# First modulation weights by feature tile: eight pieces with places of their own, four up0 units loaded early, their high parts cast on ScalarE

## The reference

```python
sc = jax.nn.silu(c)
scc = jax.nn.silu(c_ctx)
for layer in range(DEPTH):
    mod_l = (sc @ ada_w[layer] + ada_b[layer]).reshape(-1, N_MOD, D_MODEL)[:, :, None, :]
    mod_c = (scc @ ada_w[layer] + ada_b[layer]).reshape(N_MOD, D_MODEL)
    x_l = half_ffn(x_l, mod_l[:, 0], mod_l[:, 1], mod_l[:, 2], norm_g[layer, 0], ...)
    ...
def half_ffn(x, shift, scale, gate, g, w_gate, w_up, w_down):
    h = rmsnorm(x, g) * (1 + scale) + shift
    return x + 0.5 * gate * swiglu(h, w_gate, w_up, w_down)
```

## Time and profile before

| | us |
|---|---|
| median of 3 runs (lowest, highest) | 2646.4 (2646.07, 2648.47) |
| profiled execution, whole time | 2649.49 |
| profiled execution, span from first to last instruction | 2647.7 |
| TensorE busy in the span | 2518.1 (95%) |
| VectorE, ScalarE busy | 1554.8 (59%), 485.1 (18%) |
| mean transfer rate | 135 GB/s |

### The profile page before, as it was taken

One profiled execution on the slowest core, in us unless ns is written; L12 is line 12 of the kernel. 1 busy time (PEld: TensorE's weight loads), 2 busy tenths in 40 slices (PEclk: granted clock), 3 DMA queues, 4 the chain that ended last, 5 costly groups with the idle time before them and its releaser, 6 DMA issues.

```text
span 2647.7 us, 38248 instructions
## 1 busy us (share of the span) xinstructions
PE 2518.1 (95%) x15322; PEld 2142.3 (81%) x15322; DVE 1554.8 (59%) x2396; ACT 485.1 (18%) x991; POOL 5.0 (0%) x12
## 2 busy tenths in 40 slices
PE   5999999999999999999999789998999999799998
PEld 2777777877777777788888659998988999799997
DVE  4544434434644443655544637888687766679976
ACT  2000000124200000211100242111156522210001
POOL 0000000000000000000000000000000000000000
PEclk9999999999999999999999899998999999899999
DMA  5554555310354545333223204655443222346553
GB/s 206 196 183 163 178 176 192 96 32 25 124 186 161 182 167 183 104 103 96 97 94 98 82 19 127 190 179 164 163 149 107 96 65 81 120 143 187 184 185 107
DMA packets 88990, 356.81 MB, mean 135 GB/s; under 512 B 9825, under 2 KB 11105, under 8 KB 79393
## 3 DMA queue, kind: packets, MB, share of 16 engines
q1 hardware_dynamic: 86976, 349.32, 39.7%
q0 software_dynamic: 848, 4.67, 0.5%
q10 hardware_dynamic: 1040, 1.05, 0.1%
HBM read 353.95 MB, written 1.05 MB: 134 GB/s over the span
## 4 chain that ended last, share of the span: by engine, by line
PE 90%; DVE 6%; ACT 2%; DMA 2%; issue 1%; SPq 0%; DVEq 0%; ACTq 0%
PE lin L1927 24%; PE lin L1928 23%; PE lin L1929 23%; PE pair L2030 3%; PE pair L2111 2%; DMA raw_all<-w_ada 2%; PE lin L2138 1%; PE lin L1976 1%; DVE work L1500 1%; PE lin L1977 1%; PE lin L1980 1%; PE pair L2496 1%; PE pair L2483 1%; PE lin L1935 1%; PE lin L1937 1%
## 5 line engine op out<-in xcount | busy, mean ns | idle before, releaser
L1927 PE MATMUL lin<-h_all,whi 128*128 128x256 f32 (+1 forms) x2608 | 872.9, 335 | 11.1 <-DVE wlo L1423 6.1
L1928 PE MATMUL lin<-h_all,whi 128*128 128x256 f32 (+1 forms) x2608 | 860.8, 330 | 0.0
L1929 PE MATMUL lin<-h_all,wlo 128*128 128x256 f32 (+1 forms) x2608 | 860.1, 330 | 0.0
L1423 DVE TENSOR_TENSOR wlo<-raw_all,whi 128x1024 fp32r<-128x1024 f32 (+1 forms) x529 | 635.8, 1202 | 36.1 <-ACT whi L1270 19.1
L1927 PEld LDWEIGHTS lin<-h_all,whi 128*128 128x128 f32 x2608 | 497.0, 191 | 96.9 <-issue 44.9
L1422 DVE CAST whi<-raw_all 128x1024 fp32r<-128x1024 f32 (+2 forms) x489 | 330.8, 676 | 400.4 <-PE lin L1929 357.9
L1929 PEld LDWEIGHTS lin<-h_all,wlo 128*128 128x128 f32 x2608 | 497.1, 191 | 45.1
L1928 PEld LDWEIGHTS lin<-h_all,whi 128*128 128x128 f32 x2608 | 497.5, 191 | 42.6
L1927 PE MATMUL lin<-a_all,whi 128*128 128x256 f32 (+1 forms) x1148 | 388.6, 339 | 23.8 <-DVE wlo L1423 10.9
L1928 PE MATMUL lin<-a_all,whi 128*128 128x256 f32 (+1 forms) x1148 | 384.6, 335 | 0.0
L1929 PE MATMUL lin<-a_all,wlo 128*128 128x256 f32 (+1 forms) x1148 | 384.2, 335 | 0.0
(11 more groups left out here) (317 smaller groups left out, 2021.3 us busy)
## 6 DMA issues: line engine op xcount, KB each, us to landing
raw_all<-w_up SPq DMA_DIRECT2D x176, 512.0 KB, 3.5
raw_all<-w_ada SPq DMA_DIRECT2D x72, 1024.0 KB, 4.9
raw_all<-w_down SPq DMA_DIRECT2D x64, 512.0 KB, 3.5
raw_all<-w_exp_up SPq DMA_DIRECT2D x64, 512.0 KB, 3.6
raw_all<-w_exp_down SPq DMA_DIRECT2D x32, 512.0 KB, 3.5
raw_all<-w_down SPq DMA_DIRECT2D x32, 384.0 KB, 3.0
raw_all<-w_b_qk SPq DMA_DIRECT2D x24, 512.0 KB, 3.5
raw_all<-w_b_conv SPq DMA_DIRECT2D x24, 512.0 KB, 3.5
```

Source lines behind the costliest of these rows:

```text
L1423: dve.tensor_tensor(wlo[s][:, 0:n], r[:, 0:n], whi[s][:, 0:n].bitcast(F32), ALU.subtract)\
L1927: pe.matmul(out_, a, hi[n], start=start and n == 0, stop=False)
L1928: pe.matmul(out_, a, lo[n], start=False, stop=False)
L1929: ins = pe.matmul(out_, b, hi[n], start=False, stop=stop and n == len(cols) - 1)
```

## The change

Group 0 is laid out anew in HBM. Piece f (1 MB) holds, for all eight input tiles, the 128 shift columns and the 128 scale columns of feature tile f. So each piece gives the whole shift and scale of one tile. The eight pieces go to eight places in the working area that later holds the feed-forward's inner values (`first_block`), and no load of them waits. The four first up0 units go to the four places of `raw_all`, among the pieces: after piece 0 units 0 and 1, after piece 2 unit 2, after piece 5 unit 3. `x` comes in two transfers. All other pairs use the two upper places as before.

`sum_block(f)` replaces the group's sums: eight matmuls with 32 columns of weights (`cond`, padded with zeros to 32) and 256 moving columns, two in each of four groups of 32 partitions. ScalarE copies 128 x 256 (`copy_block`). `turn_block` is two matmuls that add the four partition groups and turn the row in one step (`same_row` picks the rows). VectorE makes bias and gain of the tile in two small steps (`first_modulations`). Three PSUM banks take turns, and the row buffer's two halves too. ScalarE casts the high parts of units 0 to 3 (`first_high`), VectorE makes the low parts (`first_low`), at places in the norm written out by hand.

```diff
-            sp.dma_start(x[:, :, :], dram["x_t"]).then_inc(S("x_in"), 16)
-            for p in range(8):
-                load_pair(sp, p)
+            for part, name in enumerate(("x_in", "x_rest_in")):
+                k = slice(part * KT // 2, (part + 1) * KT // 2)
+                sp.dma_start(x[:, k, :], dram["x_t"][:, k, :]).then_inc(S(name), 16)
+            for f in range(8):
+                sp.dma_start(first_block(f), dram["w_ada"][f]).then_inc(block_loaded[f], 16)
+                for j in {0: (0, 1), 2: (2,), 5: (3,)}.get(f, ()):
+                    load_unit(sp, "up0", 0, j)
...
@@ ScalarE: norm_root, norm_high, start @@
+                if src == "load":
+                    copy_block(0)
                 act.activation(small[:, 16:17], ones[:, 0:1], ACT.Sqrt)
...
                     ins.then_inc(S("h_hi_ready"), 1)
+                    if ph == "ffn0":
+                        if k == 0:
+                            first_high(2)
+                        if k + 2 < 8:
+                            copy_block(k + 2)
+                        if k == 4:
+                            first_high(3)
+            def first_high(j):
+                act.wait_ge(raw_loaded[j], 16)
+                act.activation(whi[j][:, :], raw[j], ACT.Copy).then_inc(S("first_high"), 1)
+            def copy_block(f):
+                act.wait_ge(S("block_summed"), f + 1)
+                if f >= 2:
+                    act.wait_ge(S("block_turned"), f - 1)
+                act.activation(ada_row[:, SEQ * (f % 2):SEQ * (f % 2 + 1)], block_bank(f)[:, 0:SEQ], ACT.Copy)\
+                    .then_inc(S("block_copied"), 1)
...
             norm_root("ffn0")
-            copy_modulations(0)
+            first_high(0)
+            first_high(1)
+            copy_block(1)
@@ VectorE @@
-            split("up0", 0, 0)
-            dve.wait_ge(S("params_in"), 32)
-            take_modulations(0)
-            for j in range(1, LOOK):
-                split("up0", 0, j)
+            def first_modulations(f):
+                dve.wait_ge(S("block_turned"), f + 1)
+                at = slice(f, f + KT + 1, KT)
+                src = view(block_bank(f)[:, SEQ:SEQ + 4], (2, 2))
+                link(dve.tensor_tensor(mods[:, at, :], src, P_("ada_b")[:, at].unsqueeze(2).broadcast_to([P, 2, 2]), ALU.add))
+                link(dve.scalar_tensor_tensor(gains[:, 0, f, :], mods[:, KT + f, :], 1.0,
+                                              P_("norm_g")[:, f:f + 1].broadcast_to([P, 2]), ALU.add, ALU.mult))
+                dve.sem_inc(S("block_modulated"), 1)
+            def first_low(j):
+                dve.wait_ge(S("first_high"), j + 1)
+                dve.tensor_tensor(wlo[j][:, :], raw[j], whi[j][:, :].bitcast(F32), ALU.subtract).then_inc(weights_split, 1)
+            def beside_first_norm(t):
+                if t == 0:
+                    first_low(1)
+                    first_modulations(1)
+                    first_low(2)
+                elif t < KT - 1:
+                    first_modulations(t + 1)
+                if t == 5:
+                    first_low(3)
...
+            first_modulations(0)
+            first_low(0)
@@ TensorE @@
+            def sum_block(f):
+                pe.wait_ge(block_loaded[f], 16)
+                if f >= 3:
+                    pe.wait_ge(S("block_modulated"), f - 2)
+                for half in range(2):
+                    for g in range(4):
+                        k = 2 * g + half
+                        ins = pe.matmul(block_bank(f)[32 * g:32 * g + 32, 0:SEQ], cond[:, k, :],
+                                        first_block(f)[:, SEQ * k:SEQ * (k + 1)], start=half == 0, stop=half == 1)
+                ins.then_inc(S("block_summed"), 1)
+            def turn_block(f):
+                pe.wait_ge(S("block_copied"), f + 1)
+                for m in range(2):
+                    at = SEQ * (f % 2) + P * m
+                    ins = pe.matmul(block_bank(f)[:, SEQ + 2 * m:SEQ + 2 * m + 2], ada_row[:, at:at + P], same_row[:, :],
+                                    start=True, stop=True)
+                ins.then_inc(S("block_turned"), 1)
+            def blocks_beside(k):
+                if k + 2 < 8:
+                    turn_block(k + 2)
+                if k + 3 < 8:
+                    sum_block(k + 3)
...
-            for p in range(8):
-                sum_modulations(p)
+            sum_block(0)
             norm("ffn0")
-            turn_modulations(0)
+            sum_block(1)
+            turn_block(1)
+            sum_block(2)
```

More of the change, by code:

```diff
@@ L90, in load_order @@
 def load_order():
-    order = [("pair", p) for p in range(8)]
+    order = []
     for name, n, _, _ in STREAM:
@@ L109, in load_plan @@
         if name == "pair":
-            b = j % 2 if j < 8 else 1
-            slots = (2 * b, 2 * b + 1)
+            slots = (2, 3)
         else:
-            slots = ((POSITION[name][1] + j) % 2 if name in POSITION else (FIRST[name] + j) % SLOTS,)
+            slots = (j if name == "up0" and j < 4 else (POSITION[name][1] + j) % 2 if name in POSITION else (FIRST[name] + j) % SLOTS,)
         waits = sorted({holder[q] for q in slots if holder[q]})
@@ L123 @@
 PLAN = load_plan()
-PAIR_LOADS = {p: sum(1 for o in range(p + 1) if (o % 2 if o < 8 else 1) == (p % 2 if p < 8 else 1)) for p in range(PAIRS)}
 PARAMS = [
@@ L380, in build_program, with first_block @@
         hwork = nc.alloc_sbuf_tensor_at("hwork", [P, 2 * H], F32, offset=h_at)
+        def first_block(f):
+            return work[:, H + 2048 * f:H + 2048 * (f + 1)]
         def W(at, *shape):
@@ L412, in build_program, with block_bank @@
         norm_bank = pair[1][:, 1]
+        def block_bank(f):
+            return (pair[0][:, 0], pair[0][:, 1], lin[:, 3])[f % 3]
         raw_loaded = [sem(f"raw_loaded{s}") for s in range(SLOTS)]
-        pair_loaded = [sem(f"pair_loaded{b}") for b in range(2)]
+        block_loaded = [sem(f"block_loaded{f}") for f in range(8)]
+        pair_loaded = sem("pair_loaded")
         pairs_done = sem("pairs_done")
@@ L1036, in load_region @@
                     load_pair(sp, j)
-                elif name in REGIONS[r]:
+                elif name in REGIONS[r] and (name, j) not in [("up0", u) for u in range(4)]:
                     load_unit(sp, name, j // body(name), j % body(name))
@@ L1441, in one @@
                 def one(i, j, last):
-                    if last:
+                    if stage == "up0" and i == j == 0:
+                        pass
+                    elif last:
                         split_ahead(stage, i * bs + j)
@@ L1749, in _ @@
             dve.sem_inc(inner_ready, 2)
+            dve.memset(cond[:, :, :], 0.0).then_inc(S("cond_cleared"), 1)
             dve.memset(pair[0][:, 0], 0.0).then_inc(S("sums_cleared"), 1)
-            for k in range(1, KT):
-                if k > 1:
-                    dve.wait_ge(S("squares_added"), k - 1)
-                add_squares("ffn0", k, TOK)
-            norm_mean("ffn0")
+            dve.tensor_reduce(same_row[:, :], ident.rearrange("p (g r) -> p r g", g=4)[:, 0:2], AX.X, ALU.add)\
+                .then_inc(S("row_made"), 1)
             MADE_OF = {0: ([(0, 0)], []), 1: ([], [(0, 2)]), 2: ([(0, 1)], []), 3: ([(0, 2)], []), 4: ([], [(0, 8)]),
@@ L1777, in take_modulations @@
                     link(dve.tensor_scalar(mods[:, r:r + 8, :], mods[:, r:r + 8, :], 0.5, None, ALU.mult))
[L1779 to L1783 removed]
+            def first_modulations(f):
[18 more added lines that the diff above has]
+                    first_low(3)
+            for k in range(1, KT):
+                if k > 1:
+                    dve.wait_ge(S("squares_added"), k - 1)
+                add_squares("ffn0", k, TOK)
+            norm_mean("ffn0")
+            first_modulations(0)
+            first_low(0)
             for ph in phases:
@@ L1959, in norm @@
                 ins.then_inc(S("sums_done"), 1)
+                if src == "load":
+                    turn_block(0)
                 pe.wait_ge(S("rstd_ready"), n + 1)
@@ L1968, in first_group @@
                 n = NORMS[norm_of][0]
-                slots = [ready(stage, 0, j) for j in range(FIRST_GROUP)]
-                for j in range(FIRST_GROUP):
-                    bank_free(stage, j, 0)
+                slots = [(FIRST[stage] + j) % SLOTS for j in range(FIRST_GROUP)]
                 for k in range(KT):
@@ L2023, in sum_modulations @@
                 n, k = divmod(p, 8)
-                b = p % 2 if p < 8 else 1
-                pe.wait_ge(pair_loaded[b], PAIR_LOADS[p] * 16)
-                if n and k == 0:
-                    pe.wait_ge(S("ada_copied"), n)
+                pe.wait_ge(pair_loaded, (p - 7) * 16)
+                if n == 1 and k == 0:
+                    pe.wait_ge(S("block_modulated"), 8)
+                if n > 1 and k == 0:
+                    pe.wait_ge(S("ada_copied"), n - 1)
                 for g in range(4):
-                    at = 2 * b * UNIT + 512 * g
```

(5 more changed lines are left out.)

43 lines of the change are left out of this document (26 added, 17 removed).

## The result

| | before | after |
|---|---|---|
| median of the runs, us | 2646.82 (2646.07 to 2648.47, 4 runs) | **2630.91** (2627.28 to 2634.92, 4 runs) |
| ratio to before, 95% interval | 1 | 0.9939 (0.9927 to 0.9952) |
| profiled execution, us (its span) | 2649.49 (2647.7) | 2634.92 (2632.9) |
| first piece lands | 14.11 | 14.17 |
| first matmul of up0 | 51.22 | 24.59 |

The kernel became faster by 15.9 us (0.61%). The forecast of 2631 us was met. The mark moved by 17.3 us where 15.5 were worked out, and the stretch behind it looks 2.5 us longer in this pair of traces. These are taken up in turn.

The account below looks back on a forecast made before the run. TensorE, busy 2518.1 of 2647.7 us, was taken as the bound, with room only at the start. First plain up0 unit from 71.57 to 56.1 gains 15.5: 2649.5 to 2634.0, median 3.1 lower, 2631 us; range 2625 to 2641.

Parts of the forecast that it names:

- The mark: Start of the first plain up0 unit, behind the first modulation group; forecast to move from 71.57 to 56.1 us.
- The rival of the old pace: First group's transfers: pieces still come 3.34 us apart, the last piece's sum starts 1 to 1.5 late; 2632.5 us, chance 0.03.
- Price of a sum: Summing one piece on TensorE, eight matmuls of 256 columns and 32 outputs: 1.9 us at slow clock, 1.2 at full.
- Clock at the start: TensorE before up0: slow prices (1.2 GHz) hold until the first tile's matmuls end at 29.9 us, full clock after.
- k=0: First feature tile of up0: nine matmuls at 0.43 us, from 26.1 to 29.9 us.
- Steps and stalls: First up0 group: 3.7 us per tile for turn, sum and nine matmuls, plus VectorE stalls of 1.1 and 0.7.
- x whole would do as well: Start, sum of squares: even with x in one transfer VectorE's adds ended at 17.75 us, taken as early enough.
- The casts cost nothing: First four up0 units: moving their casts from VectorE to ScalarE is free, as the sums cover ScalarE's slot.
- Slope of a dearer sum: First group: each 1 us more on a fast sum adds about 11 us, less 1.9 of swallowed stalls.
- the rival: Piece sums cost double, 3.8 us slow and 2.1 fast: 8 us lost, gain 7.5, time 2639 us; chance 0.09.
- The serial rival: Piece sums: no matmuls run side by side, 7.6 us slow and 4.2 fast; mark at 87, 2662 us; chance 0.06.
- The clock stays down: First group: TensorE stays at 1.2 GHz, 6.7 us per step; mark at 73.8, time 2648.6 us; chance 0.06.

Follow-up runs that it names:

- kernel with eight places: Kernel before, changed only so that its first eight pieces land in eight places of their own and no load waits; 2640.61 us, ratio 0.997.
- kernel with sooner turns: Against after: piece k+2 turned ahead of tile k's last matmuls, unit 3's low part made ahead of tile 6's modulation steps; 2632.40 us.
- serial run: Against after: all eight matmuls of a piece sum go to one group of 32 partitions, copy and turn read 32 rows; 2650.88 us, ratio 1.0007.
- the added matmuls: Against after: fourteen matmuls with unused results run on TensorE ahead of the first piece's sum; 2631.95 us.

## Why the prediction was right, point by point

- **The bound, and the mark as the measure**: right. TensorE's work is the same, the first 50 us gave the gain, and the shift reached the second norm whole (17.32). The kernel with eight places splits it: 6.2 us for the freed queue, 11.1 for the rest of the change.
- **Transfers**: right. The first piece at 14.17 (forecast 14.1); 416 to 424 KB per us as in the earlier trace rows, no wait on any later piece. The rival of the old pace is out, and the 2.40 to 2.50 us between pieces in the kernel with eight places say why.
- **Price of a sum**: right, 1.93 and 1.07 for 1.9 and 1.2. The choice of the row nearest by the earlier trace rows held; the end at four times that is real (3.64) if the groups aren't used. By the trace, 16 loads of 32 columns hardly show: 1.07 here, 1.04 for the eight loads of 2 columns at 53.33. The strict form of the rule in the Trainium skill, TensorE: Matmul & The Clock Gate, section on packing small matmuls, isn't borne out: these loads all use all rows, and by it they would have added an estimated 0.4 to each sum (at the columns / 1.2 ns of the same page's section on LDWEIGHTS).
- **Turn and copy**: 0.99 and 0.50 for 0.93 and 0.48; the copy 0.39 for 0.4.
- **Clock at the start**: the one term off by over a microsecond. The sum had slow prices up to 29.9. In fact the turn at 23.05 takes 0.61 and the sum at 23.59 takes 1.07: full clock before up0's first matmul, which stands at 24.59, not 26.1. The argument was that 7 us of light records had left it low before; it stretched this to all light records, and here it rose after some 8 us of them without a pause. This is 1.5 of the 1.8 us between 54.3 and 56.1.
- **k=0**: as long as forecast, 24.59 to 28.42, by luck. The matmuls took 2.7 in sum, not 3.8, but TensorE waited 1.1 for VectorE, 0.26 for unit 2's low part and 0.84 for the low part of tile 0. The forecast had the low part in time because it had TensorE slower.
- **Steps and stalls**: 3.63 for 3.7. The waits behind it are 0.81 and 0.75 for 1.1 and 0.7, and the kernel with sooner turns removes both.
- **"x whole would do as well"**: wrong. VectorE's squares then keep TensorE waiting 1.73 us. The sum itself wasn't touched by it, since x did come in halves.
- **"The casts cost nothing"**: right for what ran, but for the 0.26 that TensorE waited for unit 2's low part, whose cast stands late on ScalarE. On VectorE they would cost about 1 us, and in the execution seen 4.8 with the clock.
- **Slope of a dearer sum**: wrong. "11 us for each us more" priced the three early sums at double throughout, though with more work there the full clock came sooner in both runs (3.4 and 6.3 us behind the first piece). Doubled sums (0.86 each) cost 5.3 and not the 8 of the rival, and serial ones (2.57 each) 20.2 where the slope gives 26. The serial rival had 31 because it also took 3.0 for the 2.57. Its 2662 was 11 us too high: it measured 2650.88, which can't be told from before. The turning point "at 2.4 us" doesn't follow from the prediction's own numbers either: a gain of 15.5 and 11 us for each us, less 1.9, give 2.8. By the serial run (20.2 for 2.57) it is near 3.3, an estimate.
- **The clock stays down**: it didn't, but the danger was real. It fell again after tile 0 in two of the variants, at a price of 1.6 and some 3 us, and in one of them once more at tile 6.

The time met the forecast to 0.1 us, which is chance. By the marks alone the forecast should have been 2646.8 - 17.3 = 2629.5, and the spread of the stretch behind (2570.4 to 2578.6) is larger than this error.

## What to carry to other kernels

Where a first stage waits for all of a reduction, cut its data so that a complete part of the result comes out of each piece, and load the first consumer's data between the pieces: here the eight free places were worth 6.2 us of 17.3, and with the units behind the pieces all but 3.3 of the 17.3 were gone. A reduction on TensorE that is narrow in its outputs belongs in all four column groups (1.07 against 3.64 us for 16 records of 256 columns and 32 outputs). When a price depends on the clock, write both prices and ask what would switch it, rather than multiply the slow one by a count.

## What the runs showed of the hardware that was not expected

- **The rise of the clock.** In after, light records without a pause from 14.17 were slow to about 22.5 (the sum at 20.61 took 1.94) and then fast. With doubled sums the clock was up at 16.07 after 3.4 us of work, with serial sums at 20.71 after 6.3 us. In before, 1.89 us of work in every 3.34 left the sums at 1.89 to the last one at 37.46. With eight places, 1.89 in every 2.48 did so too, but for one sum of 1.04 at 25.96, behind which it was low again. What decides between 3 and 8 us stays open.
- **Its fall.** With short pauses ahead it fell at 28 to 31 us in two variants, x whole and the casts on VectorE (sums of 1.80 and 1.94 instead of 1.07), and not in after or its repeat, whose pauses at tile 0 are nearly the same (0.26 and 0.84; 0.26 and 0.84 with x whole, 0.74 and 0.84 with the casts on VectorE). The same at the row broadcast: behind a pause of 0.68 ahead of it, piece 1 was slow with doubled sums (3.55 for 32 records) and with the added matmuls (1.94), and fast with these and the sooner turns together (1.07).
- **The stretch behind the start** differed by up to 8 us between executions, without an edit there. The eight records of the soft-max stage that took 4.84 in before, 5.79 in after and 4.69 in its repeat, where two pauses lie ahead, show one place where this arises.
